# A hybrid mLSTM and attention layer: two gate tiles per mLSTM head instead of three, and other places for its loads and stores

## The reference

```python
u = rmsnorm(x, norm_pre_w) * (1 + scale) + shift
aq, ak, av, az, mq, mk, mv, mo, mz, mg, ga, gb = split_proj(u, w_in)
att = ...                                  # windowed attention, 16 heads
y_b = att * silu(az)
y_a, C, n, m = mlstm_branch(...)           # 4 heads x 256, two directions
merged = sigmoid(ga) * (y_a @ w_proj_a) + sigmoid(gb) * (y_b @ w_proj_b)
out = rmsnorm(merged @ w_out, norm_post_w)
return x + gate * out, (k, v, C, n, m)
```

## Time and profile before

| | us |
|---|---|
| median of 3 runs | 1956.85 |
| lowest, highest | 1956.55, 1957.27 |
| profiled execution | 1956.03 |
| its span, first to last instruction | 1954.5 |
| TensorE busy | 1920.9 |
| VectorE busy | 1204.8 |
| ScalarE busy | 667.1 |
| GpSimd busy | 113.1 |

### The profile page before, as it was taken

How to read it: one execution, slowest core, us unless ns; L and a number is a source line. 1 busy time by engine, 2 the same in 40 slices (tenths; PEclk the granted TensorE clock), 3 DMA queues, 4 the chain that set the end, 5 groups by cost and what they waited for, 6 DMA issues and landing times.

```text
span 1954.5 us, 31664 instructions
## 1 busy us (share of the span) xinstructions
PE 1920.9 (98%) x12266; PEld 1782.6 (91%) x12266; DVE 1204.8 (62%) x2073; ACT 667.1 (34%) x1015; POOL 113.1 (6%) x201
## 2 busy tenths in 40 slices
PE   6999999999999999999999999999999999999998
PEld 2589999999999999999998999889889999988886
DVE  3368766666666666665766664465556867683224
ACT  4443333333333333332555554233224222242221
POOL 2010000000000000000000000000002000000000
PEclk9999999999999999999999999999999999999999
DMA  9962353333333333334632423365454666634224
GB/s 370 399 188 82 109 166 112 113 113 113 113 113 113 113 113 113 113 113 125 185 106 83 119 78 118 91 150 135 108 130 144 201 205 184 209 116 139 80 76 161
DMA packets 297966, 274.03 MB, mean 140 GB/s; under 512 B 20128, under 2 KB 245160, under 8 KB 295968
## 3 DMA queue, kind: packets, MB, share of 16 engines
q1 hardware_dynamic: 283632, 216.71, 37.9%
q0 software_dynamic: 13952, 56.00, 7.9%
q10 hardware_dynamic: 304, 0.25, 0.0%
HBM read 235.05 MB, written 40.48 MB: 141 GB/s over the span
## 4 chain that ended last, share of the span: by engine, by line
PE 90%; DMA 4%; DVE 3%; issue 1%; SPq 1%; ACT 1%; POOL 0%; DVEq 0%; POOLq 0%; ACTq 0%
PE bank L2043 20%; PE bank L2123 12%; PE bank L2116 12%; PE bank L2117 12%; PE bank L2339 11%; PE bank L2052 10%; PE bank L1956 2%; PE bank L2243 2%; PE bank L2232 1%; PE bank L2184 1%; DMA RAW<-in_w_ada_dram 1%; PE bank L2245 1%; PE bank L2016 1%; PE bank L2161 1%; DMA Y<-in_x_prompt_dram 1%; DMA WORK<-in_w_ada_dram 1%
## 5 line engine op out<-in xcount | busy, mean ns | idle before, releaser
L2043 PE MATMUL bank<-XH,WH 128*128 128x320 f32 x1472 | 345.5, 316 | 2.8 <-DVE XL L1830 2.1
L1031 ACT ACTIVATE WH<-RAW 128x1024 fp32r<-128x1024 f32 x195 | 206.7, 1060 | 386.3 <-PE bank L2123 306.3
L2043 PE MATMUL bank<-XL,WH 128*128 128x320 f32 x1472 | 335.2, 309 | 0.0
L1465 DVE TENSOR_TENSOR WL<-RAW,WH 128x1024 fp32r<-128x1024 f32 x195 | 238.3, 1222 | 143.8 <-ACT WH L1031 143.8
L910 ACT ACTIVATE WH<-RAW 128x1024 fp32r<-128x1024 f32 x122 | 129.1, 1059 | 530.8 <-PE bank L2052 406.4
L2043 PEld LDWEIGHTS bank<-XH,WH 128*128 128x128 f32 x1472 | 244.5, 188 | 10.8 <-issue 8.0
L2043 PEld LDWEIGHTS bank<-XL,WH 128*128 128x128 f32 x1472 | 246.2, 188 | 0.0
L2052 PE MATMUL bank<-XH,WL 128*128 128x320 f32 x1472 | 235.9, 310 | 0.0
L2052 PEld LDWEIGHTS bank<-XH,WL 128*128 128x128 f32 x1472 | 220.1, 188 | 4.1 <-issue 3.8
L2117 PE MATMUL bank<-XL,WH 128*128 128x320 f32 x720 | 212.5, 309 | 0.0
L2116 PE MATMUL bank<-XH,WH 128*128 128x320 f32 x720 | 212.4, 309 | 0.0
(11 more groups left out here) (243 smaller groups left out, 2962.3 us busy)
## 6 DMA issues: line engine op xcount, KB each, us to landing
RAW<-in_w_in_dram SPq DMA_DIRECT2D x165, 512.0 KB, 3.8
WORK<-in_w_ada_dram SPq DMA_DIRECT2D x70, 512.0 KB, 8.5
proj_dram<-OUTS POOLq DMA_DIRECT2D x92, 320.0 KB, 2.5
RAW<-in_w_out_dram SPq DMA_DIRECT2D x32, 512.0 KB, 3.8
RAW<-in_w_ada_dram SPq DMA_DIRECT2D x26, 512.0 KB, 9.3
WORK<-proj_dram SPq DMA_DIRECT2D x16, 640.0 KB, 4.4
WORK<-proj_dram POOLq DMA_DIRECT2D x32, 320.0 KB, 3.3
RAW<-in_w_proj_a_dram SPq DMA_DIRECT2D x16, 512.0 KB, 4.6
```

The costliest lines, as they stand in the source:

```text
L1031: ins = nc.scalar.activation(WH[:, (j + p) % 2, :], pair_raw(j, p), ACT.Copy)
L1465: V.tensor_tensor(WL[:, w, :], pair_raw(j, p), WH[:, w, :].bitcast(F32), ALU.subtract)\
L2043: pe.matmul(banks[n][:, 0:HALF_TOK], wh[:, k, :], x[:, k0 + k, n * HALF_TOK:(n + 1) * HALF_TOK], start=(first and k == 0 and wi == 0), sto ...
```

## The change

- `T_L1` and `T_L2` move by four tiles: 32 pairs in place of 30, and two plain tiles for each mLSTM head in place of three. The loops of the stage go over thirds of a half (16 matmuls each), so a head keeps its 12 phases.
- The backward state product moves from phase 10 to 11, the transposes of the output rows from 11 to 12, the writing of Y from 11 to 12; the copy of the backward state stands ahead of the normalisation.
- `HH` and the output gate (`MG`) get memory of their own; rows are loaded after the queries were scaled (`ml_qs`), keys after the context product (`ml_sp`), the gate without waiting for `ml_kw`.
- Each direction has its store semaphore and its stores; SP's order around them changes.
- The merge takes the attention's half first: w_proj_b and Y rows 8 to 15, with high parts ahead of the last head's Y and five low parts (`LOW_EARLY`) ahead of its writing. The first four merge halves are issued in the loop.
- The descriptor memory of GpSimd's DMAs is set to 4096.

```diff
-T_PAIR, T_L1, T_L2, T_MERGE, T_OUT, T_END = 4, 64, 78, 90, 106, 122
+T_PAIR, T_L1, T_L2, T_MERGE, T_OUT, T_END = 4, 68, 82, 90, 106, 122
-L1_TILES, L2_TILES = 14, 3
+L1_TILES, L2_TILES = 14, 2
+LOW_EARLY = 5
...
+        HH = sb("HH", [P, 5, MD])
+        MG = sb("MG", [P, 2, TOK])
...
-            def states_out(h):
-
-                for r, there in enumerate((ml_upd, ml_cbd)):
-                    sp.wait_ge(there, h + 1)
-                    for cc in range(2):
...
+            def state_out(h, r):
+
+                sp.wait_ge((ml_upd, ml_cbd)[r], h + 1)
+                for cc in range(2):
+                    sp.dma_start(new_C[0, 0, r, h, cc * P:(cc + 1) * P, :], CA[:, r, cc, 0:MD])\
+                        .then_inc(ml_state_out[r], 16)
+                    sp.dma_start(new_n[0, 0, r, h, cc * P:(cc + 1) * P].rearrange("(p o) -> p o", o=1),
+                                 CA[:, r, cc, MD:MD + 1]).then_inc(ml_state_out[r], 16)
...
-                    sp.wait_ge(ml_zg, h)
+                    sp.wait_ge(ml_sp, h)
                 head_rows(h, MK, RB_MK, ml_kv)
...
-                    sp.wait_ge(ml_ht, h)
+                    sp.wait_ge(ml_qs, h)
...
-            for s in range(2 * L2_TILES * M_HEADS):
-                if s > 6 and s % 6 == 4:
-                    row_loads(s // 6)
-                in_tile(T_L2 + s // 2, 0, COL_MERGE + P * (GATES_PAIRED + L1_TILES + s // 2), (s % 2,))
+            for s in range(2 * L2_TILES * M_HEADS + 4):
+                if s < 2 * L2_TILES * M_HEADS:
+                    in_tile(T_L2 + s // 2, 0, COL_MERGE + P * (GATES_PAIRED + L1_TILES + s // 2), (s % 2,))
+                else:
+                    merge_half(0, (s - 16) // 2, s % 2)
                 for h in range(M_HEADS):
-                    if s == (3 if h == 0 else 6 * h + 3):
+                    if s == 4 * h + 3:
                         if h == 0:
                             head_values(0)
-                        head_keys(h)
-                        if h:
+                            head_keys(0)
+                        else:
+                            row_loads(h)
+                            head_keys(h)
+                            state_out(h - 1, 0)
+                            state_out(h - 1, 1)
                             head_queries(h)
-                    if s == 6 * h + 4:
+                    if s == 4 * h + 4:
                         if h == 0:
                             head_queries(0)
                             row_loads(0)
-                        if h:
-                            states_out(h - 1)
...
+                        else:
+                            state_loads(h)
+                            if h + 1 < M_HEADS:
+                                head_values(h + 1)
...
                     if r == 10:
+                        dve.wait_ge(ml_cb, h + 1)
+                        for cc in range(2):
+                            ins = V.tensor_copy(CA[:, 1, cc, :], ab[2 + cc][:, 0:257])
+                        ins.then_inc(ml_cbd, 1)
                         dve.wait_ge(ml_rs, h + 1)
...
-                    if r == 11:
+                    if r == 12:
                         dve.wait_ge(ml_ht, h + 1)
...
-                if part and s + 1 < 2 * L2_TILES * M_HEADS:
+                if part == 1 and s + 1 < 2 * L2_TILES * M_HEADS:
                     lo(0, 0, 2 * T_L2 + s + 1)
+                if q == 6 * L2_TILES * M_HEADS - 2:
+                    low_y(range(LOW_EARLY), y_hi, y_lo, 8)
...
-            low_y(range(3), y_hi, y_lo)
+            low_y(range(LOW_EARLY, 8), y_hi, y_lo, 8)
             lo(0, 0, 2 * T_MERGE)
-            low_y(range(3, 8), y_hi, y_lo)
+            low_y(range(8, 12), y_hi, y_lo, 8)
             lo(0, 0, 2 * T_MERGE + 1)
-            low_y(range(8, KT), y_hi, y_lo)
+            low_y(range(12, KT), y_hi, y_lo, 8)
...
-                    high_products(banks, w, 8 * x, range(0, 4), x == 0)
-                else:
-                    high_products(banks, w, 8 * x, range(6, 8), x == 0)
+                    high_products(banks, w, 8 * x, range(0, 3), x == 0)
+                elif part == 1:
+                    high_products(banks, w, 8 * x, range(4, 7), x == 0)
+                else:
                     pe.wait_ge(lo_done, 2 * t + x + 1)
-                    low_products(banks, w, 8 * x, x == 1, range(0, 4))
+                    low_products(banks, w, 8 * x, x == 1, range(0, 6))
```

More of the change, by code:

```diff
@@ L419, in hybrid_layer @@
                              "ml_sp", "ml_pp", "ml_w", "ml_qs", "ml_kw"))
-        ml_uf, ml_ufd, ml_ub, ml_ubd, ml_up, ml_upd, ml_cb, ml_cbd, ml_state_out = (
-            sem(n) for n in ("ml_uf", "ml_ufd", "ml_ub", "ml_ubd", "ml_up", "ml_upd", "ml_cb", "ml_cbd", "ml_state_out"))
+        ml_uf, ml_ufd, ml_ub, ml_ubd, ml_up, ml_upd, ml_cb, ml_cbd = (
+            sem(n) for n in ("ml_uf", "ml_ufd", "ml_ub", "ml_ubd", "ml_up", "ml_upd", "ml_cb", "ml_cbd"))
+        ml_state_out = [sem(f"ml_state_out{r}") for r in range(2)]
         ml_var, ml_rs, ml_h, ml_ht, ml_eg, ml_zg, ml_v, ml_ya = (
@@ L720, in out_piece @@
                 w_half(8 * n + (g - 3), g, g % 4, w_out_v[:, 2 * q:2 * q + 2, bass.ds(512 * n, 512)], k=2)
[L722 to L725, removed]
+            for r in range(2):
+                state_out(M_HEADS - 1, r)
             sp.wait_ge(ml_ya, M_HEADS + 1)
-            sp.wait_ge(ml_state_out, 128 * M_HEADS + 16)
+            for r in range(2):
+                sp.wait_ge(ml_state_out[r], 64 * M_HEADS)
             with sp.Fori(0, 7) as i:
@@ L747, in _ @@
             sp.wait_ge(kv_out, 16 * 8 + 16)
-            sp.wait_ge(ml_state_out, 16 * 8 * M_HEADS + 16)
+            for r in range(2):
+                sp.wait_ge(ml_state_out[r], 64 * M_HEADS)
         @block.gpsimd
@@ L872, in _ @@
             merge_gates(1, 1)
-            pool.wait_ge(ml_state_out, 128 * M_HEADS + 16)
+            for r in range(2):
+                pool.wait_ge(ml_state_out[r], 64 * M_HEADS)
             nc.gpsimd.memset(GS, 0.0).then_inc(filled, 1)
@@ L1166, in inter @@
                 nc.scalar.activation(ENM[:, :, :], COLH[:, :, 2:4], ACT.Exp).then_inc(ml_w, 1)
-            for q in range(4 * L2_TILES * M_HEADS):
-                s, part = divmod(q, 2)
+            for q in range(6 * L2_TILES * M_HEADS):
+                s, part = divmod(q, 3)
                 if part == 0:
@@ L1688, in _, with low_y @@
                         low_keys(kv, 3)
-            dve.wait_ge(m0_in, 16)
+            def low_y(ks, high, done, shift=0):
+                for k in ks:
+                    dve.wait_ge(high, k + 1)
+                    V.tensor_tensor(XL[:, k, :], Y[:, (k + shift) % KT, :], XH[:, k, :].bitcast(F32),
+                                    ALU.subtract).then_inc(done, 1)
             def small(h):
@@ L2309, in _ @@
                 if part == 0:
-                    high_products(banks, w, 8 * x, range(4, 6), x == 0)
-                else:
-                    low_products(banks, w, 8 * x, x == 1, range(4, 8)).then_inc(w_used, 1)
-            pe.wait_ge(ml_ya, M_HEADS + 1)
+                    high_products(banks, w, 8 * x, range(3, 4), x == 0)
+                elif part == 1:
+                    high_products(banks, w, 8 * x, range(7, 8), x == 0)
+                else:
+                    low_products(banks, w, 8 * x, x == 1, range(6, 8)).then_inc(w_used, 1)
             def merge_tile(i, u, k_wait):
```

64 lines of the change are left out of this document (25 added, 39 removed).

## The result

The changed kernel takes 1986.24 us (median of 5 runs, 1984.69 to 1988.55) against 1956.85 before: a ratio of 1.015, 95% interval 1.014 to 1.0161. It is slower by 29.4 us; 1984 was predicted, 1957 to 1999. The profiled execution has a span of 1984.7 us, 30.2 more than before, and a mean granted clock of 0.992.

What follows compares the result with a forecast made beforehand. TensorE, busy nearly the whole span, was taken as the bound. Terms -7.04 + 1.25 + 3 x (1.7 + 6.1 + 2.3) + 2.5 = +27.0 us on 1956.03 gave 1983.0, median 1984, range 1957 to 1999.

Steps and rivals of the forecast that it cites:

- two more pairs: Pair stage: four gate tiles move from plain tiles into two more pairs, 7.04 us less TensorE work.
- head 0, key-query wait: First mLSTM head: TensorE ready 8.35 us into the stage, VectorE's copies at 9.5; wait 1.25 us, once.
- VectorE's chain to Y: Each mLSTM head: from the prompt products' result until Y is written, 15.7 us.
- transposes behind Y: The next head's first transposes wait for Y, which uses the same banks: 1.7 us, three times.
- stores issued: SP issues eight state stores from T + 48.4 to 53.7, T being the start of a head's first transposes.
- queries issued, there: Queries go out behind eight state stores at T + 54.9, land T + 66 (T: start of head's first transposes).
- key-query products: Heads 1 to 3: TensorE waits for late queries, then masks and copies; 6.1 us a head, ends 4 and 9.
- half clock: TensorE's clock falls to half during the key-query wait and returns as slowly: 2.3 us a head, three times.
- merge's first tile: Merge start: TensorE waits for VectorE's z products, low parts and Y; loss 5.9 against 3.36, 2.5 us more.
- Rival B: Same waits as the main forecast, but the clock stays up: +20.1 us, 1977; chance 0.20.
- rival C: Queries aren't held by the stores and land 4.4 us after issue: +1.8 us, 1958.6, no difference; chance 0.12.
- rival D: Faster: the removed work counts, VectorE keeps up and queries land by then needed: 1951.8; chance 0.13.

Runs made afterwards that it cites:

- the kernel with the queries ahead: Changed kernel with the sigmoid of z in other memory and queries issued with the keys, ahead of the eight state stores: 1959.28 us, ratio 1.0017.
- the order alone in the kernel before: Kernel before the change with one thing moved: queries issued behind the eight state stores instead of ahead: 1999.41 us, ratio 1.0218.
- without the large stores: Changed kernel without the sixteen 128 KB stores of the new C state, the 4-byte n stores kept ahead of the queries: 1977.97 us, ratio 1.0112.
- the low part behind Y: Changed kernel with queries issued ahead of the stores, plus VectorE's weight low part moved from a pass's middle third to its last: 1961.19 us, ratio 1.0027.

## Why the prediction was right

With T = 1266.73 for the head whose state is stored, the steps can be laid beside the trace.

| step | predicted | seen |
|---|---|---|
| two more pairs | -7.04 | -7.04, then 1.1 lost on the way: the stage begins at 1264.38, not 1263.3 |
| head 0, key-query wait | 1.25 | 0.90 |
| VectorE's chain to Y | 15.7 | 15.9 |
| transposes behind Y | 3 x 1.7 | 3 x 1.78 |
| stores issued | T + 48.4 to 53.7 | T + 49.7 to 55.8 |
| queries issued, there | T + 54.9, T + 66 | T + 56.0, T + 68.2 |
| key-query products | T + 70, wait 6.1 | T + 72.2, wait 6.85; 19.1 for three |
| half clock | 3 x 2.3 | 6.8 for three |
| merge's first tile | 2.5 | 3.0, of which 0.9 by half clock in the low products |

The sum of the right column: -7.04 + 1.1 + 0.9 + 5.3 + 19.1 + 6.8 + 3.0 = 29.2 us of the 30.2 by which the span grew. A head's undisturbed period explains the rest: 67.24 - 1.78 - 6.85 - 2.17 = 56.4 against the 56.2 predicted, four times. The 1.1 us ahead of the stage can't be put down to the change: in the traces of the other versions, whose code is the same up to there, the first transposes come between 1264.96 and 1266.67, here at 1266.73.

The key-query wait came out so close because both sides of it were late. The queries landed 2.2 us later than summed, and TensorE was ready for the products at T + 65.4, not at T + 63.9. Two sums of the prediction are off by a little: the copies at 9.5 and TensorE at 8.35 make a wait of 1.15 for head 0, not 1.25, and its own rows give 1.5 for the wait for Y, not 1.7.

The half clock, row by row: from key-query products to read-outs 14.18, 14.75 and 13.94 us in heads 1 to 3 against 12.01 in the kernel with the queries ahead, together 6.84. That the return lasts as long as the fall was a guess without a row behind it, as the prediction says. By the mean it came out right; single heads lost from 1.93 to 2.74. Rival B (the clock stays) is refuted by the 0.50 of the window above, rival C (the queries aren't held) by their 12.2 us and by the order alone in the kernel before, rival D by the waits for Y.

The merge came as described: VectorE is through with z, takes five low parts from 1523.30, and TensorE, done at 1522.4, waits twice.

```profile
1524.27 0.53 PE L2055 MATMUL bank<-XH,WH 128*128 128x320 f32 x2 [1.89 <-DVE XL L1704]
...
1529.68 0.57 PE L2055 MATMUL bank<-XH,WH 128*128 128x320 f32 x2 [1.72 <-DVE XL L1704]
...
1532.39 3.43 PE L2064 MATMUL bank<-XH,WL 128*128 128x320 f32 x16
...
1540.35 2.51 PE L2064 MATMUL bank<-XH,WL 128*128 128x320 f32 x16
```

Two things in the reasoning were not right, though the number didn't suffer. I wrote that what is queued behind the stores "on the same queue" waits; the kernel with the small stores on ScalarE's queue shows that other queues wait too, and more. And the 1.1 us before the stage and the 0.2 a head were not in the sum. One thing stays open: why the loads issued around four stores of 512 bytes land only after 9 to 21 us was not taken apart further, whether by the number of their descriptors or by where they are written.

## What to carry to other kernels

When a step moves past others in a DMA queue, list what it then stands behind, and price the slowest of these by its landing, not its bytes: here one swapped line was worth 43 us in the old kernel and 24.5 in the new. Put loads that someone waits for ahead of stores of a few bytes a partition, in the same queue, and early: directly ahead, one load in each of two versions landed only after 13.6 and 13.2 us; with 15 us of room no wait for them was left. Moving these stores to a second queue made it worse here. When cover is cut (three tiles a head to two), look at the engine that was hidden: VectorE is busy for only 62%, and still TensorE now waits for it 1.8 us a head. An operation moved out of its way is felt by whatever waits for its semaphore, here SP's queue.

## What the runs showed of the hardware

The loss by the clock did not grow with the wait. The key-query products (16 of 512 columns, 7.03 us at 2.4 GHz) took 8.75 after a wait of 3.71 us and 8.83 after 4.06 (without the large stores), 9.96 after 3.85 (the low part behind Y), 9.19, 9.77 and 8.97 after 6.85, 6.72 and 5.50 (the changed kernel), and 9.86, 8.56 and 8.89 after 12.39, 11.24 and 12.73 (the order alone in the kernel before). After the wait of 0.90 us they took 7.13. So a wait of some 4 us on TensorE cost some 6 here, and one of 12 some 14.

```profile
1399.10 8.75 PE L2242 MATMUL bank<-WORK 128*128 128x512 f32 x16 [3.71 <-DVE WORK L1717]
```
